# In the loop over pairs of experts, TensorE turns the next pair's gathered rows ahead of the down matmuls

## The reference

```python
    comb = (jax.nn.one_hot(g_idx[:, 0], MOE_GROUPS, dtype=F32)[:, :, None]
            * (g_w[:, :, None] * in_group[:, None, :]))
    ...
    for g in range(MOE_GROUPS):
        a = jax.nn.silu(jnp.einsum('nd,edf->nef', x, wg4[g])) * jnp.einsum('nd,edf->nef', x, wu4[g])
        a = a * comb[:, g, :, None].astype(a.dtype)
        y = y + jnp.einsum('nef,efd->nd', a, wd4[g]).astype(F32)
```

## Time and profile before

| | us |
|---|---|
| median of three runs | 1278.49 (1277.01 to 1285.94) |
| the profiled execution | 1279.06 |
| its span | 1277.3 |
| TensorE busy with matmuls | 998.0, 78% of the span |
| VectorE busy | 438.6, 34% |
| ScalarE busy | 239.8, 19% |
| GpSimd busy | 109.4, 9% |
| gate and up matmuls (L972) | 250.9 in 1024 instructions |
| down matmuls (L992) | 115.8 in 512 instructions |
| the 32 gathers (L634) on GpSimd | 1.0 each |
| the 32 scatters (L640) on GpSimd | 1.0 each |

### The profile page before, as it was taken

How to read it: one execution, slowest core, us unless ns; L and a number is a source line. 1 busy time by engine, 2 the same in 40 slices (tenths; PEclk the granted TensorE clock), 3 DMA queues, 4 the chain that set the end, 5 groups by cost and what they waited for, 6 DMA issues and landing times.

```text
span 1277.3 us, 14064 instructions
## 1 busy us (share of the span) xinstructions
PE 998.0 (78%) x5638; PEld 559.1 (44%) x5638; DVE 438.6 (34%) x973; ACT 239.8 (19%) x512; POOL 109.4 (9%) x137
## 2 busy tenths in 40 slices
PE   4899799966679749987788168999996698787770
PEld 3555544756575533333333044566744333333320
DVE  1327202466982431111111144788434211111114
ACT  2034001322310301111111121223312011111111
POOL 0400000000000001111110300000000011111110
PEclk8899998887889859998889669999997699998995
DMA  9656675472539517999996812002376299999943
GB/s 359 207 184 212 256 290 184 166 274 75 203 145 388 224 47 319 425 423 426 426 425 290 298 54 79 1 1 95 120 313 247 79 388 425 424 426 425 425 181 155
DMA packets 84276, 321.90 MB, mean 252 GB/s; under 512 B 10448, under 2 KB 14032, under 8 KB 59376
## 3 DMA queue, kind: packets, MB, share of 16 engines
q1 hardware_dynamic: 67680, 287.29, 56.5%
q0 software_dynamic: 14752, 28.86, 6.5%
q10 hardware_dynamic: 1776, 4.81, 1.0%
HBM read 313.26 MB, written 28.62 MB: 268 GB/s over the span
## 4 chain that ended last, share of the span: by engine, by line
PE 54%; DMA 26%; DVE 14%; issue 3%; ACT 1%; SPq 1%; POOL 0%; DVEq 0%; POOLq 0%; ACTq 0%; PEldq 0%
PE bank L736 24%; DMA ARENA<-in_moe_w_up 16%; PE bank L972 10%; PE bank L992 4%; DMA ARENA<-h_dram,ARENA 4%; PE bank L823 3%; PE bank L844 2%; PE bank L762 2%; PE bank L1092 2%; DMA ARENA<-in_even_w_in 2%; PE bank L744 2%; DMA ARENA<-y_dram 1%; DMA y_dram<-GATE,ARENA 1%; PE bank L871 1%; DMA ARENA<-in_mod_w 1%
## 5 line engine op out<-in xcount | busy, mean ns | idle before, releaser
L972 PE MATMUL bank<-ARENA 128*64 128x512 f32 x1024 | 250.9, 646 | 58.7 <-DMA ARENA<-in_moe_w_up 51.0
L736 PE MATMUL bank<-ARENA,hT 128*128 128x512 f32 (+3 forms) x480 | 187.8, 552 | 10.9 <-DMA ARENA<-in_even_w_in 7.8
L972 PEld LDWEIGHTS bank<-ARENA 128*64 128x64 f32 x1024 | 83.2, 149 | 205.0 <-issue 189.7
L736 PEld LDWEIGHTS bank<-ARENA,hT 128*128 128x128 f32 x480 | 92.5, 195 | 101.3 <-issue 80.5
L1714 DVE TENSOR_TENSOR ARENA<-bank,ARENA 128x256 f32<-128x256 f32 x32 | 13.6, 425 | 308.5 <-ACT ARENA L1277 308.5
L992 PE MATMUL bank<-ARENA 128*64 128x512 f32 x512 | 115.8, 592 | 1.2 <-ACT ARENA L1293 1.2
L992 PEld LDWEIGHTS bank<-ARENA 128*64 128x64 f32 x512 | 39.7, 137 | 70.5 <-issue 68.8
L736 PE MATMUL bank<-hT,ARENA 128*128 128x384 f32 x192 | 65.0, 501 | 5.9 <-DVE hT L1839 5.2
L640 POOL DMA_INDIRECT y_dram<-GATE,ARENA x32 | 32.0, 998 | 409.9 <-PE bank L961 269.9
L762 PE MATMUL bank<-ARENA,cond 128*32 128x128 f32 x1536 | 52.2, 293 | 18.2 <-DMA ARENA<-in_mod_w 17.0
L1277 ACT ACTIVATE ARENA<-bank 128x256 f32<-128x256 f32 x32 | 12.3, 384 | 287.3 <-PE bank L972 287.3
(11 more groups left out here) (286 smaller groups left out, 1106.1 us busy)
## 6 DMA issues: line engine op xcount, KB each, us to landing
ARENA<-in_moe_w_gate SPq DMA_DIRECT2D x32, 2048.0 KB, 25.5
ARENA<-in_moe_w_up SPq DMA_DIRECT2D x32, 2048.0 KB, 31.1
ARENA<-in_moe_w_down SPq DMA_DIRECT2D x32, 2048.0 KB, 24.6
ARENA<-in_mod_w SPq DMA_DIRECT2D x24, 2048.0 KB, 10.2
ARENA<-in_even_w_in SPq DMA_DIRECT2D x6, 2048.0 KB, 14.8
y_dram<-ARENA POOLq DMA_DIRECT2D x2, 3072.0 KB, 22.6
ARENA<-y_dram SPq DMA_DIRECT2D x6, 1024.0 KB, 8.5
GATE<-mod_dram POOLq DMA_DIRECT2D x8, 512.0 KB, 5.6
```

The costliest lines, as they stand in the source:

```text
L736: last = nc.tensor.matmul(out, lhs(c), rhs(c), start=(c == 0), stop=(c == chunks - 1))
L972: last = nc.tensor.matmul(banks[2 + i % 2][64 * e:64 * e + 64, :], XGT[:, c, 64 * e:64 * e + 64], w[:, e, :, c, :], start=(c == 0), stop=( ...
```

## The change

In each pass of the loop the turn of the next pair's rows changes places with the down matmuls: TensorE's program becomes gate_up(i), turn(i+1), down(i-1), turn_act(i). On ScalarE and VectorE `copy_x(i+1)` and `copy_y(i-1)` change places in the same way. In the first pass (i = 0) there is no down, and in the last no turn, so these two are as before. GpSimd's and SP's programs are not touched.

```diff
@@ -996,10 +996,10 @@
                 turn(0)
                 for i in range(PAIRS):
                     gate_up(i)
+                    if i + 1 < PAIRS:
+                        turn(i + 1)
                     if i:
                         down(i - 1)
-                    if i + 1 < PAIRS:
-                        turn(i + 1)
                     turn_act(i)
                 down(PAIRS - 1)
 
@@ -1296,10 +1296,10 @@
                 copy_x(0)
                 for i in range(PAIRS):
                     gate_silu(i)
+                    if i + 1 < PAIRS:
+                        copy_x(i + 1)
                     if i:
                         copy_y(i - 1)
-                    if i + 1 < PAIRS:
-                        copy_x(i + 1)
                     copy_act(i)
                 copy_y(PAIRS - 1)
 
```

## The result

| | before | after |
|---|---|---|
| median of the runs, us | 1277.76 (4 runs, 1277.01 to 1285.94) | 1399.3 (4 runs, 1392.99 to 1406.61) |
| the profiled execution, us | 1279.06 | 1397.22 |
| its span, us | 1277.3 | 1395.4 |

The ratio of after to before is 1.094, with a 95% interval of 1.0879 to 1.1001: slower. The prediction was 1402 us with a range of 1345 to 1430. All ratios here are formed from a kernel's faster executions alone, so they need not equal the quotient of the medians.

The account below looks back on a forecast made before the run. Weight transfers at 16.0 us per pair were taken to bound the loop; a new cycle of 18.3 us plus 2.1 of half clock would replace them, adding 122.6 us to 1279.1: 1402 us, range 1345 to 1430.

Parts of the forecast that it names:

- The cycle: Loop over expert pairs: down releases the next gather, whose turn now precedes the next down; one trip per pair sets the rate.
- The rival that gathers become quick: With DMA engines partly idle, gathers land under 8.5 us, weights still bound the loop, time stays 1279; chance 0.05.
- The trip: Turn 1.0, down 3.55, path to the gather's start 2.9, gather 10.8: 18.3 us per pair, plus 2.1 for the clock.
- The clock: TensorE drops to half clock after each wait of about 6 us, slowing turn and down by 2.1 us per pair.
- the rival of a clock that stays up: The cycle closes, but turn and down run at 2.4 GHz: 1351 us; chance 0.09.
- The last gather: Gather 15, with only one 2 MB load left to issue, lands in 6 us, 4.8 less than the others.
- The loops: The expert-pair loops take 60.4 us more in layer 0 and 62.2 us more in layer 1.
- The rest was taken as unchanged: What follows each loop (scatters, results back, combining) takes the same time as before.
- Costs put at nothing: Down's result copies lie within the 2.9 us counted, copy_x ahead of copy_y delays nothing, weights come in time.
- the gain of the copies' wait: L972's waits for VectorE's copy of turned rows, 23.0 us in all, vanish; worth nothing in pairs bound by weights.
- Faster: Gathers keep up and weights do not bind, so the copies' wait is saved: 1256 us at best; chance 0.02.

Follow-up runs that it names:

- e1: The changed kernel with the copies' order on ScalarE and VectorE taken back, so only TensorE's order is new: 1406.96 us, ratio 1.1004 to the kernel before.
- e3: The changed kernel with GpSimd issuing each gather one place earlier, gather(i+3) ahead of scatter(i): 1280.46 us, ratio 0.9987 to the kernel before.
- e7: The changed kernel with 6 unneeded matmuls between gate_up(i) and the wait of turn(i+1), i from 2 to 13: 1343.58 us, ratio 1.0507 to the kernel before.
- e2: The kernel before with only the copies' order on ScalarE and VectorE changed, TensorE's order as before: 1280.89 us, ratio 1.0019.
- e4: The kernel before with GpSimd issuing each gather one place earlier: 1278.19 us, ratio 0.9999.
- e8: The changed kernel without its 32 scatters, only counted as landed (outputs wrong): 1310.93 us, ratio 1.0228 to the kernel before.
- e5: The changed kernel loading weights of only three pairs per layer (outputs wrong): 1201.57 us, ratio 0.9392 to the kernel before.
- e6: The kernel before, loading weights of only three pairs per layer (outputs wrong): 1204.28 us, ratio 0.9442 to the full kernel before.
- e10: The kernel before with weights of only three pairs per layer (outputs wrong), timed longer: 1201.26 us, ratio 0.9417 to the full kernel before.
- e9: The changed kernel with weights of only three pairs per layer (outputs wrong), timed longer: 1201.68 us, ratio 0.9389 to the kernel before.

## Why the prediction was right, and where its terms were off

- *The cycle.* Right: down releases the next gather, and TensorE's order alone closes the cycle (e1), an earlier issue alone opens it (e3). The rival that gathers become quick with the DMA engines idle part of the time fell: 10.2 us at a busy share of 0.78. Load batch and gather are released by the same down, so the busy share is 1.01 while the gather is on its way, and the engines idle after it.
- *The trip.* Predicted 18.3 us plus 2.1 of clock, 20.4; measured 20.62 and 20.51. The fixed part was a little too large (e7, at full clock, has 18.0 and 18.2) and the clock too small. End of down to the gather's start is 2.92 us (505.13 to 508.05) as taken. The 24 gathers ahead of turns 3 to 14 took 10.02 to 11.52 us, 10.45 in the mean, 10.8 taken. At full clock down starts 1.09 us after the turn, not 1.0 (480.11 and 479.02 in the profile after).
- *The clock.* Predicted that the turn goes from 1.15 to 1.95 us (measured 1.97) and down loses 1.3 (2.1 less the turn's 0.8); down took 4.84 to 5.65 us, 5.24 in the mean, 1.6 more. In all 2.4 us instead of 2.1, and each of the 24 long waits brought it: the rival of a clock that stays up is not what happened. The five rows it was taken from the earlier trace rows had waits of 4.1 to 4.2 us; waits here were 5.5 to 7.0. That the longer wait is what makes the clock stay down longer is not shown.
- *The last gather.* Put at 6 us beside a single load; 734.11 to 740.33 us is 6.2. It was put between two rows without a row of its own, so some luck is in it.
- *The loops.* Predicted +60.4 and +62.2 us; measured 303.2 instead of 238.9 (457.47 to 760.69 us) and 300.6 instead of 236.4 (1057.09 to 1357.71): +64.3 and +64.2. Together 5.9 us more than the sum's 122.6.
- *The rest was taken as unchanged* and came out 10 us shorter: the loop of layer 0 began at 457.47 us instead of 470.53. The programs are the same up to there, and over all the runs the two starts don't go with the order of turn and down (last section), so nothing ties this to the change. That the 5.9 us too few in the loops and these 10 us too many partly cancelled is luck: 1402 predicted, 1399.3 measured. Against the execution that the sum was made from, 122.6 us were predicted and 118.1 found in the span: 128.5 in the loops, 10.4 less elsewhere.
- *Costs put at nothing* were nothing: the copies' order by itself (e2, ratio 1.0019), the weights (no wait of L972 for them in the kernel after), and the gain of the copies' wait as long as weights bind (e4 and e3 equal).
- *A misreading that the sum did not use.* The 23.0 us in 31 waits for VectorE's copy add the waits of PEld (15.3 us) to the matmuls' (7.7 us in 14 waits). The rival *Faster* had 1256 us at best from it; with the matmuls' own waits it is 1271.

## What to carry to other kernels

Before moving a step ahead of another, follow what the later step releases, through the queues of the other engines, to the input of the moved one. Where a step now waits for something that the step behind it sets free, the latency of that path becomes the rate of the loop; here a queue entry one place earlier would have kept it out. A transfer's latency is to be read from a row with the traffic that will be beside it, and the clock that a wait costs counts only if what runs behind the wait is in the cycle.

## What the runs showed of the hardware

- A gather of 128 rows of 4 KB took 3.3 us to land with the DMA engines quiet, 8.5 beside weight loads, and 10.2 beside weight loads and behind a scatter (medians of e8 and of the profile after). Behind a scatter but without weight loads it took 3.4 (e5). That the DMA engines idled for a fifth of each trip changed nothing of it: the idle time lay behind the gather.
- After a wait of 5.5 to 7.0 us a turn of eight transposes took 1.97 us and the down behind it 4.8 to 5.7 instead of 3.65; after 1.6 to 1.7 us (turn 15 of both layers) both were at full clock. In between the length of the wait alone did not decide: in e8 five of the 24 trips kept the full clock in turn and down, after waits of 2.20 to 2.51 us, while after 2.17 us (588.96 us) the turn took 1.16 us and the down behind it 5.35, and after 2.28 us (1142.13 us) 1.16 and 5.32.
- The stage ahead of the loops differed between the profiled executions by more than many changes are worth: the loop of layer 0 began at 470.53 us in the profile of before and at 457.47 to 462.13 in those of after, e1 to e4, e6, e7 and e10, but at 470.5 to 472.0 again in e5, e8 and e9, although the programs of these kernels are the same up to there. In the stretch from 210 to 280 us the granted clock is 0.85 in the profile of before and 0.91 in that of after:

```profile
210.00:280.00 70.00, 63.15 (x649) 45.84 (x647) 33.45 (x88) 16.06 (x60) 5.50 (x10) 0.85 0.61 216
```
```profile
210.00:280.00 70.00, 56.14 (x653) 43.44 (x654) 38.73 (x91) 22.10 (x63) 4.91 (x8) 0.91 0.67 241
```

The late starts (e5, e8, e9) have 0.83 to 0.85 there, too, and the early ones 0.91 to 0.94, but for e7, which has 0.82 and still began at 461.83 us. So the clock of this stretch goes with the start in most of the profiles and is not shown to be its cause. The new order of TensorE is found with both starts (after and e5), and so is the old one (e6 and before). The two pairs that were profiled twice, e5 and e9, e6 and e10, agree within 1 us each, so it is open whether the start goes with the kernel or with the execution.
